# Two transformer blocks on one core: z projections moved into the inverse's tail, convolution taps as a step of their own, and another order of the output products

## The reference, cut to what matters

```python
def first_block(...):                              # 16 meta tokens + 256 tokens
    u = rms_norm(h, norm_mix_pre)
    dq, dk, dv, dz, db, da, aq, ak, av = split(u @ w_in)
    o_dn = gated_deltanet_group(dq, dk, dv, dz, db, da, ...)
    o_at = axial_gqa_group(aq, ak, av, ...)
    h = h + rms_norm(concat([o_dn, o_at]) @ w_out)
    u = rms_norm(h); f = square(relu(u @ w_up)) @ w_down; h = h + rms_norm(f)

def gated_deltanet_group(q, k, v, z, b, a, ...):
    q, k, v = split(short_conv_silu(concat([q, k, v])))   # 5 taps in time
    ...
    uw = triangular_solve(a_low + I, rhs)   # here: the inverse, from 8x8 blocks up to 128x128
    ...                                     # a scan over chunks, o_n and o_i
    return rms_norm(o) * silu(z)
```

## Time and profile before

| | |
|---|---|
| median of 3 runs | 1128.24 us (1124.64 to 1128.39) |
| the profiled execution | 1129.35 us, of which the span is 1127.6 us |
| PE busy | 1069.7 us (95%) |
| DVE, ACT, POOL busy | 634.7, 562.4, 157.3 us |
| mean granted clock of TensorE | 0.974 |
| chain of waits | PE 84%, DVE 8%, ACT 4%, issue 2%, POOL 1% |

### The profile page before, as it was taken

How to read it: one execution, slowest core, us unless ns; L and a number is a source line. 1 busy time by engine, 2 the same in 40 slices (tenths; PEclk the granted TensorE clock), 3 DMA queues, 4 the chain that set the end, 5 groups by cost and what they waited for, 6 DMA issues and landing times.

```text
span 1127.6 us, 17744 instructions
## 1 busy us (share of the span) xinstructions
PE 1069.7 (95%) x7413; PEld 970.2 (86%) x7413; DVE 634.7 (56%) x954; ACT 562.4 (50%) x1007; POOL 157.3 (14%) x128
## 2 busy tenths in 40 slices
PE   6997998999999999988899999999999999999997
PEld 5887977889989897987679999997999879999996
DVE  4696932477554547158876544546533456544544
ACT  6653243266453536654445543444766665443442
POOL 1040002000000000776330000000232210000000
PEclk9998968999999999999899999999999999999999
DMA  7332100054646555443234546545443334546541
GB/s 257 113 112 75 63 15 1 1 163 155 205 153 219 160 216 178 141 149 113 75 112 169 195 157 208 200 152 187 127 140 113 112 112 168 197 152 213 195 151 66
DMA packets 114975, 160.42 MB, mean 142 GB/s; under 512 B 3776, under 2 KB 99136, under 8 KB 114896
## 3 DMA queue, kind: packets, MB, share of 16 engines
q1 hardware_dynamic: 114896, 159.29, 42.3%
HBM read 158.23 MB, written 1.05 MB: 141 GB/s over the span
## 4 chain that ended last, share of the span: by engine, by line
PE 84%; DVE 8%; ACT 4%; issue 2%; POOL 1%; DMA 0%; SPq 0%; DVEq 0%; POOLq 0%; ACTq 0%
PE PS L643 23%; PE PS L645 22%; PE PS L644 22%; ACT SCR L1367 3%; PE PS L956 1%; DVE WL L1798 1%; PE PS L961 1%; PE PS L1328 1%; PE PS L677 1%; DVE SCR L2290 1%; PE PS L1351 1%; PE PS L1249 1%; PE PS L1339 1%; POOL SM L2363 1%; DVE SPARE L1798 1%
## 5 line engine op out<-in xcount | busy, mean ns | idle before, releaser
L1367 ACT ACTIVATE WH<-RAW 128x1024 fp32r<-128x1024 f32 (+1 forms) x191 | 194.9, 1048 | 48.1 <-DMA RAW<-in_gu 26.9
L1798 DVE TENSOR_TENSOR WL<-RAW,WH 128x1024 fp32r<-128x1024 f32 (+1 forms) x149 | 180.5, 1242 | 59.1 <-ACT WH L1367 58.8
L643 PE MATMUL PS<-UH,WH 128*128 128x256 f32 (+2 forms) x664 | 188.7, 284 | 4.2 <-DVE WL L1798 3.0
L1367 ACT ACTIVATE SCR<-PS 128x512 f32<-128x512 f32 (+8 forms) x233 | 101.3, 469 | 182.7 <-PE PS L645 122.2
L645 PE MATMUL PS<-UH,WL 128*128 128x256 f32 (+2 forms) x664 | 188.0, 283 | 0.0
L644 PE MATMUL PS<-UL,WH 128*128 128x256 f32 (+2 forms) x664 | 187.9, 283 | 0.0
L1798 DVE TENSOR_TENSOR SPARE<-RAW,SPARE 128x1024 fp32r<-128x1024 f32 x100 | 118.0, 1220 | 22.5 <-ACT SPARE L1367 22.5
L643 PEld LDWEIGHTS PS<-UH,WH 128*128 128x128 f32 (+1 forms) x664 | 124.8, 188 | 6.3 <-DVE WL L1798 3.5
L645 PEld LDWEIGHTS PS<-UH,WL 128*128 128x128 f32 (+1 forms) x664 | 124.9, 188 | 0.5
L644 PEld LDWEIGHTS PS<-UL,WH 128*128 128x128 f32 (+1 forms) x664 | 124.3, 187 | 1.1
L2363 POOL TENSOR_TENSOR SM<-SM 128x1 f32<-128x1 f32 (+5 forms) x32 | 26.1, 815 | 662.9 <-DVE SM L1809 625.7
(11 more groups left out here) (303 smaller groups left out, 2220.1 us busy)
## 6 DMA issues: line engine op xcount, KB each, us to landing
RAW<-in_gu SPq DMA_DIRECT2D x44, 1024.0 KB, 5.2
RAW<-in_dn SPq DMA_DIRECT2D x22, 1024.0 KB, 6.7
RAW<-in_w_up SPq DMA_DIRECT2D x16, 1024.0 KB, 6.4
RAW<-in_w_down SPq DMA_DIRECT2D x16, 1024.0 KB, 5.0
RAW<-in_a_qkv SPq DMA_DIRECT2D x12, 1024.0 KB, 5.2
RAW<-in_w_in SPq DMA_DIRECT2D x11, 1024.0 KB, 5.3
RAW<-in_kv_w SPq DMA_DIRECT2D x8, 1024.0 KB, 6.1
RAW<-in_w_out SPq DMA_DIRECT2D x4, 1024.0 KB, 4.9
```

The costliest lines, as they stand in the source:

```text
L643: e.matmul(o, lh, rh, start=start, stop=False)
L1367: return e.activation(o, i, func, bias=bias, scale=scale, accum_out=acc)
L1798: e.tensor_tensor(lo_of(n_), half_src(n_), hi_of(n_).bitcast(F32), SUB).then_inc(s_lo_dve, 1)
```

## The change

1. **STAGE_1.** `z.0` and `z.1` no longer stand around `solve`; `conv.4` stands before `solve`, `conv.5` behind it. All four z steps now stand among `inv.12`, `meta.6`, `in`, `inv.13` and `inv.14`. They take PSUM banks 4 and 5 in turn, and the tile of z is loaded behind those of `conv`.
2. **Taps.** DVE's taps are now a step `taps.i` of its own. `taps.5` stands behind `inv.2`, `meta.2` and `inv.3`; the others stand directly behind their `conv`.
3. **vtok.0** moves from ahead of `rows.1` and `inv.7` to behind both. `qp.2` moves ahead of `gqa.2`.
4. **STAGE_2.** No z step is left behind the scan. `og.4` to `og.7` run together ahead of the transposes of `on.5`, and all four halves for the scan's result are one `out_last`.
5. **Splits.** In the stretches between (with an MLP behind them) two more halves are split inside the features (`ah.4`, `ah.5`). In STAGE_3 and STAGE_4, `o.4` and `o.5` split two halves more than before, so `o.6` has two fewer. `head` and `spare_free` are set to match.

```diff
-    "meta.0 q.0 q.1 inv.0 meta.1 inv.1 q.2 q.3 q.4 rows.0 z.0 solve z.1 conv.4 inv.2 conv.5 inv.3 meta.2 inv.4 conv.6 inv.5 "
-    "meta.3 conv.7 inv.6 silu.1 vtok.0 rows.1 inv.7 meta.4 conv.8 inv.8 rows.2 conv.9 inv.9 vtok.1 vtok.2 inv.10 conv.10 "
-    "meta.5 inv.11 conv.11 inv.12 meta.6 silu.2 in.0 inv.13 in.1 gqa.0 inv.14 qp.0 gqa.1 qp.1 gqa.2 qp.2 gqa.3")
+    "start.0 start.1 meta.0 q.0 q.1 inv.0 meta.1 inv.1 q.2 q.3 q.4 rows.0 conv.4 solve conv.5 inv.2 meta.2 inv.3 taps.5 inv.4 "
+    "conv.6 inv.5 meta.3 conv.7 taps.7 inv.6 silu.1 rows.1 inv.7 vtok.0 meta.4 conv.8 inv.8 rows.2 conv.9 taps.9 inv.9 vtok.1 "
+    "vtok.2 inv.10 conv.10 meta.5 inv.11 conv.11 taps.11 inv.12 z.0 meta.6 silu.2 in.0 z.1 inv.13 in.1 z.2 inv.14 z.3 gqa.0 "
+    "qp.0 gqa.1 qp.1 qp.2 gqa.2 gqa.3")
...
-    " on.0 z.2 on.1 z.3 on.2 og.4 on.3 og.5 on.4 og.6 on.5 og.7 on.6")
+    " on.0 on.1 on.2 og.4 on.3 og.5 on.4 og.6 og.7 on.5 on.6")
...
-    "fe.1.0 fe.1.1 fe.1.2 fe.1.3 fe.1.4 fe.1.5 fe.1.6 fe.1.7")
+    "fe.1.0 fe.1.1 fe.1.2 fe.1.3 ah.4 fe.1.4 fe.1.5 fe.1.6 fe.1.7 ah.5")
...
-                head = (0, 1, 4, 5, 2, 3, 6, 7, 4, 5)[:8 + (b - a) % 8]
+                head = (4, 5, 6, 7, 0, 1, 2, 3) if r == 2 else (4, 5, 0, 1, 2, 3, 6, 7, 4, 5)
...
-        z_bank = (4, 5, 2, 3)
+        z_bank = (4, 5, 4, 5)
...
-            for k in range(2):
-                out_half(1, half_of(("out", 1, 0), k), k, mix_ready(1, k), False)
-            out_last(1, [half_of(("out", 1, 1), j) for j in range(2)], [2, 3], [mix_ready(1, 2), mix_ready(1, 3)])
+            out_last(1, [half_of(("out", 1, k // 2), k % 2) for k in range(4)], range(4), [mix_ready(1, k) for k in range(4)])
...
+            def next_halves(r):
+
+                return lambda k: ahead(LAST_OUT[r] + 1 + k - AHEAD) if r + 1 in MLP else None
...
-                return lambda i: ahead(half_of(("out", r, i // 2), i % 2) if i < 6 else LAST_OUT[r] + 1)
+                return lambda i: ahead(half_of(("out", r, i // 2), i % 2) + (2 if i >= 4 else 0))
...
             def conv(i):
                 ahead(HALF_CONV[i])
-                if i % 2 == 0:
-                    return
+
+            def taps(i):
```

More of the change, by code:

```diff
@@ L216, in program @@
             w_rows(("q", k), win, 4 * k, 4, 2064, 512)
-        w_cols(("z", 0), win, 1536, 256)
         for b in (4, 5, 0, 1):
             w_cols(("conv", b), win, 256 * b, 256)
-        w_cols(("z", 1), win, 1792, 256)
+        for k in range(2):
+            w_cols(("z", k), win, 1536 + 256 * k, 256)
         for k in (2, 3, 0, 1):
@@ L585, in program @@
         spare_free = {}
-        for r, early, late in ((2, gq_p["g"], mx_lo[1, 3]), (4, dt_p[3, 1], dh_u[7]), (6, None, sh_u[15])):
-            for i, x in ((2, early), (3, early), (6, late), (7, late)):
-                spare_free[MLP_AT[r][0] + i] = x
+        for r, early, i, late in ((2, gq_p["g"], 2, mx_lo[1, 3]), (4, dt_p[3, 1], 6, dh_u[7]), (6, None, 6, sh_u[15])):
+            for j in range(2):
+                spare_free[MLP_AT[r][0] + j], spare_free[MLP_AT[r][0] + i + j] = early, late
         block = ctx.enter_context(nc.Block())
@@ L1417, in fe @@
                         ).then_inc(*uhi.step((r, x, c, k)))
-                in_order(BETWEEN if r < 6 else BETWEEN_LAST, dict(sq=sq, hs=hs, xn=xn, fe=fe))
+                in_order(BETWEEN if r < 6 else BETWEEN_LAST, dict(sq=sq, hs=hs, xn=xn, fe=fe, ah=next_halves(r)))
+            def next_halves(r):
+                return lambda k: ahead(LAST_OUT[r] + 1 + k - AHEAD) if r + 1 in MLP else None
             def second_target():
@@ L1850, in between, with next_halves @@
                 in_order(BETWEEN if r < 6 else BETWEEN_LAST,
-                         dict(mx=mx, ad=ad, xn=xn, fe=fe, r0=lambda c: root_sum(r, c, 0), r1=lambda c: root_sum(r, c, 1)))
+                         dict(mx=mx, ad=ad, xn=xn, fe=fe, r0=lambda c: root_sum(r, c, 0), r1=lambda c: root_sum(r, c, 1), ah=next_halves(r)))
+            def next_halves(r):
+                return lambda k: ahead(LAST_OUT[r] + 1 + k - AHEAD) if r + 1 in MLP else None
             def second_target():
@@ L2223, in on @@
                                                ).then_inc(*mx_lo.step((1, h)))
-            in_order(STAGE_1, dict(gqa=gqa, ba=ba, gates=gates, conv=conv, kv=kv, q=q, z=z, ktok=ktok, vtok=vtok, start=start, inv=inv, meta=meta,
+            in_order(STAGE_1, dict(gqa=gqa, ba=ba, gates=gates, conv=conv, taps=taps, kv=kv, q=q, z=z, ktok=ktok, vtok=vtok, start=start, inv=inv, meta=meta,
                                solve=solve, qp=qp, rows=rows))
```

## The result

The changed kernel takes 1145.05 us (median of 4, 1142.46 to 1146.52), the kernel before 1126.44 beside it. The ratio is 1.0165, with a 95% interval of 1.0131 to 1.0198. It is slower by 18.6 us, where 1132.1 and a range up to 1140 were forecast. The profiled execution has a span of 1144.2 us, 16.6 more than that of the kernel before, whose profiled execution (1129.35 us) lies 2.9 us above its own median here.

What follows compares the result with a forecast made beforehand. PE was taken to bound the kernel, busy 1069.7 of 1127.6 us. The seven terms summed to +3.9 us, giving 1133.2 for the profiled execution and 1132.1 us against the median, range 1121.5 to 1140.

Steps and rivals of the forecast that it cites:

- term 3: Inverse's tail: four z steps moved in cost +4.7 us, net of a filled `qp.2` wait and regained clock.
- terms 5 and 6: Extra splits delay `o.6` in STAGE_3 (+0.7 us) and `o.5` in STAGE_4 (+0.9 us), each net of MLP relief.
- term 7: Half clock behind the longer waits of the change: +1.0 us, bounds 0 and +4.
- Terms 1 and 2: Around `solve`, z steps gone: -4.0 us; `vtok.0` behind `rows.1` and `inv.7`, so `meta.4` waits: +3.8 us.
- two thirds: In the tail, the share of the possible 7.9 us clock gain that z steps would bring: 5.3 us.
- rival (a): z products keep the tail at 2.4 GHz, rounds 3 and 5 lose nothing: total +0.3, 1128.5 us; chance 28%.
- rival (b): Tail from 148 us to the scan's start stays at 1.2 GHz despite z steps: +9.2, 1137.4 us; chance 22%.
- a tail near 1.00: Sign that the prediction is wrong: the granted clock in the inverse's tail near 1.00.
- Term 4: Behind the scan: `z.2` and `z.3` go, but waits for ML of 1.1 and 0.9 us appear: -3.2 us.

Runs made afterwards that it cites:

- vtok_back: The changed kernel with `vtok.0` back ahead of `rows.1` and `inv.7`: 1135.81 us, ratio 1.0103 to the kernel before.
- before_warm: The kernel before with idle products alone, ahead of `meta.2`, `vtok.0` and `qp.2`: 1116.80 us, ratio 0.9919.
- late_splits: The changed kernel with `o.4` and `o.5` of STAGE_3 and STAGE_4 splitting as before, `ah.4` and `ah.5` kept: 1135.83 us, ratio 1.0088.
- joined: The changed kernel with `vtok.0` and the splits in `o.4` and `o.5` as before, and `meta.6` ahead of `z.0`: 1125.60 us, ratio 1.0008.
- the fastest kernel here: `joined` with `z.2` and `z.3` behind the scan again and idle products ahead of `meta.2`, `qp.2` and `gqa.3`: 1115.32 us, ratio 0.9909.

## Why the prediction was wrong

The sign was right, and most mechanisms. The size was not: +3.9 was forecast and +16.6 came in the profiled execution. Two steps failed, the filling of the wait at `qp.2` (term 3) and the chain behind the two splits (terms 5 and 6). The clock behind waits was too cheap in term 7, and the scan's had no term.

**Terms 1 and 2 were right.** `meta.2` starts at 85.86 (forecast 85.6), `inv.3` takes 3.68 us (3.6), `conv.6` starts 3.9 us earlier (4.0). `meta.4` waits 5.84 us (5.7), until 115.69 (115.7), and `inv.8` starts at 121.34 (121.0). Together +0.2, forecast -0.2. One thing that this sum did not see: the kernel with `vtok.0` moved back was 7.0 us faster, not 3.8. In its trace 6.0 us are there by `meta.6`, since `inv.7` took 3.74 us behind the wait of 2.27 and not the 5.37 that I had put down to that wait; the rest is the clock farther on.

**Term 3 failed in one step: "The wait of 2.8 us at `qp.2` is filled by z steps and the new order".** Nothing filled it. The chain that is waited for begins with a score product of PE (L1160, at 179.25), goes over DVE's maximum and ACT's exponential and copy, and lets PE go on at 183.99, 3.5 us behind the product's end. ACT's timeline has its second half:

```profile
182.30 0.58 ACT L1366 ACTIVATE SCR<-PS,SM 128x272 f32<-128x272 f32 x1 [5.19 <-DVE SM L2179]
```

All z steps stand ahead of `gqa.0`, so they are over before this chain begins, and nothing stands inside it. `qp.2`, moved ahead of `gqa.2`, meets a wait of its own: ACT's square of q stands behind the exponentials of `gqa.0`, which `inv.14` no longer covers. So it is 1.24 + 2.64 = 3.9 us instead of 2.8. ACT's part of a z step is one copy of 0.38 us and does not make the wait: without `z.2` and `z.3` it was 1.31 + 2.22.

The term came to +8.2 for +4.7, and this step is 3.6 of the difference of 3.5, the rest nearly cancelling: the four z steps cost 4 x 3.08 = 12.3 at full clock (forecast 11.6), the wait for the taps 1.49 (1.3). The waits of the tail come to 4.4 us with the 0.56 ahead of `gqa.0`, before to 3.6, so +0.8 where I had -2.8. What remains of the sum is the clock, which gave back a little more than I took: 12.3 + 1.5 + 0.8 - 8.2 = 6.4 us for my 5.3. That these are near is partly luck. The factor of 1.44 came from `inv.7`, which ran only partly at half clock; L976 took 3.31 us before and 1.90 now, a factor of 1.74. And the row from 113.1 to 116.4 that I read as `conv.8` is `inv.7`: `conv.8` started at 118.04, at full clock. So the argument for two thirds, against rival (a) and for rival (b), had no row. I had also called a tail near 1.00 a sign of being wrong; it was at 1.00 for 18.5 us, and the gain went into the z steps' own work and the waits.

**What had no term: the scan's clock.** +3.7 us. Before, the scan is at full clock from 181.3 on the earlier trace rows, 3.5 us behind its start. In the changed kernel it is at 0.52 until 198.0. With both waits at the tail's end filled, nothing of it is left: from the first products of the scan to `gt` PE takes 47.43 us in all three kernels that have this, and 48.91 in the kernel before. But the waits' length does not give the price. The changed kernel takes 52.57, `vtok_back` with the same two waits 48.91, and `before_warm` 52.57 with only 0.26 us of wait left there. No run filled these two waits alone; but between them and `meta.4` stand 18.5 us at 1.00, which speaks for them. My rival (b) ended its reckoning at "the scan's start", and so could not see it. By the rule of the Trainium skill (TensorE: Matmul & The Clock Gate, Part 1: The HAM clock gate) that I cited for the longer waits at `meta.2` and `meta.4`, the waits of the tail's end had to be weighed as well. The changed kernel's trace agrees with it: 0.50 to 0.52 behind each of them, and 1.00 once they are filled. `before_warm` does not: its scan starts at 0.50 behind hardly any wait.

**Term 4 was right:** waits of 1.02 and 1.01 us for ML (1.1 and 0.9), 0.15 for the split (0.5), and in all -2.8 up to `keep_warm` and another -0.6 at the first features, -3.4 for the forecast -3.2.

**Terms 5, 6 and 7 were mis-sized:** +0.7, +0.9 and +1.0 forecast, +5.2 and +3.9 measured (6.0 and 4.7 us from place to place in the table, less 0.8 each for the gain in the MLP), the clock included. Here the changed kernel's DVE ahead of `nb.3`, which answers to the earlier trace rows:

```profile
584.27 3.73 DVE L1801 TENSOR_TENSOR SPARE<-RAW,SPARE 128x1024 fp32r<-128x1024 f32 x2 [1.41 <-ACT SPARE L1366]
587.91 0.68 DVE L2288 TENSOR_TENSOR SCR<-SCR 128x512 f32<-128x512 f32 x1
588.63 0.69 DVE L2290 TENSOR_REDUCE SM<-SCR 128x4 f32<-128x512 f32 x1
589.23 1.22 DVE L1801 TENSOR_TENSOR WL<-RAW,WH 128x1024 fp32r<-128x1024 f32 x1
591.63 1.14 DVE L2297 SCALAR_TENSOR_TENSOR SCR<-SCR,SM,ROWS 128x128 f32<-128x128 f32 x4 [1.18 <-POOL SM L2370]
```

The failed step is "now the pair ends at about 580.4, POOL's norm root (1.3) behind it gives 581.8". Less the 7.7 us by which everything is late here, the pair ends at 580.3, as I said. But L2288 and L2290 (1.4 us), which POOL needs, stand behind the pair, and POOL takes 2.2 us, not 1.3: its L2515 takes 1.10 us beside DVE's next split, 0.20 before. L2297 starts, on the same count, at 583.9. I had also let PE be free until `o.6`; the wait is one step earlier, in `nc.3`, and PE was there at 588.4 with nothing to do. In STAGE_4 the pair takes 3.68 us, not 2.5, beside POOL's split of 2.36, and `o.5` waits 4.35 us instead of 3.2. The clock behind both waits costs 2.3 and 2.1 us, where term 7 had 1.0 for all. The gains of 0.8 us at each MLP came. They can be told apart: from `keep_warm` behind `w_out` to the end PE takes 871.6 us before, 868.2 in `late_splits` and in `joined`, and 878.9 in the changed kernel. The splits moved into the features are worth 3.4 us; those moved into the output products cost 10.7.

So of the 12.7 us by which the sum was too small, 3.5 are term 3, 3.7 the scan's clock and 6.5 the two places of the splits with their clock (5.2 + 3.9 - 2.6). The first mixer's other terms make 0.2, and about 1 us the other way are small shifts in STAGE_3, in a stretch where the change moves nothing.

What stays open: where the clock falls behind a given wait, and for how long, could not be read from the traces beforehand, and differs between kernels with the same waits. For the first mixer I have no sum that holds in every trace.

## What to carry to other kernels

Price a wait of the bounding engine twice: by its length, and by the work behind it at half clock, up to 20 us of it here and at times none. Before work is moved into or out of a wait, try idle products in that wait; here they alone gave 0.8%, and the change took 1.65%. Work that is to fill a wait has to stand inside it, behind the instruction that starts the awaited chain: the z steps stood ahead of it, and the wait stayed. And when work is moved ahead of a short chain over three engines, add up the whole chain behind it, with durations from where two of them work at once.

## What the hardware showed that I had not expected

- DVE is slowed when POOL splits too. DVE's split is 1.23 us alone and 3.12 us beside POOL's; a pair of them takes 3.68 and 3.73 us for 2.39. POOL's own split takes 2.54 us for 2.40. The excess (1.9, 1.3 and 1.3 us) is nearly the time that both ran together (2.0, 1.45 and 1.5), so DVE all but stood still in it. Here is POOL beside the pair shown above:

```profile
583.37 2.40 POOL L2366 TENSOR_TENSOR WL<-RAW,WH 128x1024 fp32r<-128x1024 f32 x1 [3.27 <-ACT WH L1366]
```

  The Trainium skill (GPSIMD Engine Reference, 1. Specifications) says that POOL shares its SBUF interfaces with VectorE, with contention for DVE instructions that read two inputs from SBUF, as a split does; the rows agree.
- The same instructions of the first mixer do not always get the same clock. In the kernel with part 5 alone, whose program is that of before up to the first MLP, the inverse's product L976 and the small ones behind it ran at 0.93, while they are in the stretch at 0.50 in the earlier trace rows, and `keep_warm` started at 250.50 instead of 255.98:

```profile
152.00:157.00 5.00, 4.46 (x34) 2.81 (x32) 0.00 (x0) 2.67 (x6) 0.00 (x0) 0.93 0.00 0
```

- So one profiled execution of such a kernel is uncertain by some 5 us, and a forecast that starts from it should say so. Here it did not: against the trace of that kernel the changed one is 14.8 us later at `keep_warm`, not 9.3, and part of the 6.4 us of clock that term 3 gave back is gained in some executions without any z step. The executions of the kernel before span 9 us, those of the fastest kernel here 1.6; of the kernel before with its waits filled, six lie within 2.6 us and one 8 us above them.
